# Cross attention in rounds of two query tiles on unnormalised queries, the forget chain inside a branch projection, the output turned chunk by chunk, and six fewer filler products in a climb

## The chip, the cores and the metric

The kernel runs on one core of a Trainium2 chip. Five engines work side by side, each through its own instruction list, and hold each other back with semaphores only: TensorE (PE, matrix products and transposes into the PSUM banks; its weight loads are PEld), VectorE (DVE), ScalarE (ACT), GpSimd (POOL) and SyncE (SP, which issues the loads). The metric is the device time of one execution in microseconds (us), as the median of several runs; lower is better.

## The reference

A two-layer decoder trunk over 512 tokens of width 1024, in float32. A layer adds three things to x: the gated sum of four token mixers, a cross attention into 256 memory rows, and a SwiGLU feed-forward part. Each is RMS-normalised before and after. What the change touches is this:

```python
def rmsnorm(x, g):
    xf = x.astype(jnp.float32)
    y = xf * lax.rsqrt(jnp.mean(xf * xf, axis=-1, keepdims=True) + NORM_EPS)
    return (y * g.astype(jnp.float32)).astype(x.dtype)

def fox_mixer(q, k, v, f_logit, f_bias):      # one of the four mixers
    log_f = jax.nn.log_sigmoid(f_logit.astype(jnp.float32) + f_bias.astype(jnp.float32))
    cum = jnp.cumsum(log_f, axis=1)
    return causal_block_attention(q, k, v, HEAD_DIM ** -0.5, cum)   # scores + cum[t] - cum[s]

def memory_cross_attention(h, mem_n, w_q, w_kv, w_o):
    B, S, _ = h.shape
    M = mem_n.shape[1]
    q = (h @ w_q).reshape(B, S, XA_HEADS, HEAD_DIM)                 # 4 heads of 64
    kv = (mem_n @ w_kv).reshape(B, M, 2, XA_HEADS, HEAD_DIM)
    s = jnp.einsum('bshd,bmhd->bhsm', q, kv[:, :, 0]).astype(jnp.float32) * HEAD_DIM ** -0.5
    p = jax.nn.softmax(s, axis=-1)
    o = jnp.einsum('bhsm,bmhd->bshd', p.astype(kv.dtype), kv[:, :, 1])
    return o.reshape(B, S, XA_HEADS * HEAD_DIM) @ w_o

for l in range(DEPTH):
    h = rmsnorm(x, mix_norm_pre[l])
    ...   # four mixers, fox_mixer the last of them
    merged = sum(jax.nn.sigmoid(h @ w_gate[l, i]) * (y @ w_branch[l, i]) for i, y in enumerate(branches))
    x = x + rmsnorm(merged @ w_out[l], mix_norm_post[l])
    hx = rmsnorm(x, xa_norm_pre[l])
    y = memory_cross_attention(hx, rmsnorm(mem, xa_mem_norm[l]), xa_w_q[l], xa_w_kv[l], xa_w_o[l])
    x = x + rmsnorm(y, xa_norm_post[l])
    ...   # SwiGLU part, its norms and residual
return x
```

## The kernel before

**Data.** The residual stream lies in `trunk` with features on partitions: eight chunks of 128 features by 512 tokens. Every float32 product is made of three products of rounded parts (high by high, low by high, high by low; `product`), so whatever enters a product is first split: ACT writes the rounded high part (`w_hi`, `h_hi`, `q_tile`, `p_hi`, `y_hi`), DVE then the difference (`w_lo`, `h_lo`, `p_lo`, `y_lo`).

**Weights.** All projections are cut into units of 128 by 1024 weights. SP loads a unit into one of two slots of `w_f32`; `next_unit(name, k)` on ACT and on DVE splits the unit that follows unit k of that name (the lists of all units are one sequence). A slot is split again only once PE has used the unit two before. PE accumulates in two banks `acc`, in turn, and a bank has to be read before it is written again. The order of PE, of ACT and of DVE is written out by hand, engine by engine; each runs strictly in that order.

**Climb.** `climb` is the stretch in which a residual is being added chunk by chunk (DVE: scale, add, then the low part; ACT: the high part and the square) while PE already projects the chunks that are ready: first unit of chunk kt, second unit of chunk kt-2, and the sums of squares (`chunk_sums`, products with one column). `keep_busy(n)` puts n products of 128x512 with no use between them. There are six climbs; the one of layer 0's first norm goes by another path (`paired_sums`).

**Cross attention.** It is the pass `XA` of `attend`: 16 steps, a head by a tile of 128 queries each. A step is: scores (PE, 3 products of 256 columns), bias and row minimum in one DVE operation, exp with row sum (ACT), reciprocal and division (DVE), two transposes (PE), high part (ACT), low part (DVE), application to the values (PE, 6 products of 128 columns). Ahead of it the norm's factor is spread over 128 rows (`spread_rows`), copied (`copy_rows`), multiplied into the projected queries (`by_rows`, into `proj_x`), and those are split (`stage`). The queries are negated, so a row's minimum takes the place of its maximum.

**Forget chain.** After the projection `fox` and ahead of its attention, DVE and ACT make the running sums of log sigmoid: eight DVE operations and, on ACT, an exp and a log, on 8 rows of 512. ACT then splits a weight unit and the first head.

**Branch.** `branch(b)` multiplies a mixer's output by w_branch in four units of two chunks; DVE, per unit, makes the next unit's `w_lo`, and twice takes a bank times the gate (bank free from here) and adds it to `trunk`.

**Output.** At the end `trunk` is turned to token order in eight half tiles (a tile of tokens needs all eight chunks), ACT copies each, SP writes out a tile of tokens (512 KB, rows of 4 KB) at a time.

## Time and profile before

| | |
|---|---|
| time, median of 3 runs | 2554.49 us (2554.11 to 2559.22) |
| the profiled execution's own time | 2556.63 us |
| its span, first to last instruction | 2554.9 us |
| PE busy | 2436.2 us, 95% of the span |
| DVE busy | 1507.8 us, 59% |
| ACT busy | 1138.6 us, 45% |
| POOL busy | 113.7 us, 4% |
| mean granted TensorE clock | 0.983 of full speed |

The span is taken from one profiled execution; its own time is 1.7 us above the span. PE is busy nearly all the time, so the stretches in which it isn't, or works without use, are what other orders can win or lose.

### The profile page before, as it was taken

To read this page: it belongs to the slowest core of one execution; us is meant where nothing else is said; L and a number is where in the kernel's file an instruction comes from. 1 tells how busy PE (TensorE), PEld (TensorE's weight loads), DVE (VectorE), ACT (ScalarE), POOL (GpSimd) and SP (SyncE) were. 2 spreads that over 40 slices of the span, in tenths; PEclk is the share of its full clock that TensorE was granted. 3 is DMA by queue.
4 is the path that set the end of the run, shared out by engine and by line. 5 is a ranking of instruction groups with operands and counts; after the bars stand their busy time and mean duration, and the time that the engine had idled before them with its cause. 6 is when DMAs were issued, how large, how long until landed. Compare 5 with 4: busy or idle time off the path is not lost.

```text
span 2554.9 us, 37831 instructions
## 1 busy us (share of the span) xinstructions
PE 2436.2 (95%) x13433; PEld 2015.8 (79%) x13433; DVE 1507.8 (59%) x3235; ACT 1138.6 (45%) x2267; POOL 113.7 (4%) x179
## 2 busy tenths in 40 slices
PE   6998999999999899999999999999999998999998
PEld 4887787888878688888878877878878787888886
DVE  5668776772775555552275786768447556555422
ACT  4456564643545532222243565646346445222322
POOL 3000000000001100000010000000000101000000
PEclk8999999999999999999999999999999999999999
DMA  5321122123124023333332212221321320333332
GB/s 120 91 91 34 50 67 67 59 62 95 42 81 134 28 64 92 97 98 91 89 83 71 79 34 58 67 67 50 83 74 50 124 74 26 91 99 98 95 91 70
DMA packets 343961, 193.99 MB, mean 76 GB/s; under 512 B 29825, under 2 KB 339206, under 8 KB 343174
## 3 DMA queue, kind: packets, MB, share of 16 engines
q1 hardware_dynamic: 340512, 178.02, 24.4%
q0 software_dynamic: 2224, 13.67, 1.5%
q8 instruction: 90, 1.47, 0.2%
q10 hardware_dynamic: 1078, 0.36, 0.1%
q14 instruction: 57, 0.47, 0.1%
HBM read 184.69 MB, written 7.34 MB: 75 GB/s over the span
## 4 chain that ended last, share of the span: by engine, by line
PE 82%; DVE 8%; ACT 4%; issue 4%; POOL 1%; DMA 0%; DVEq 0%; POOLq 0%; ACTq 0%
PE acc L1272 62%; PE o_acc L1272 5%; PE turn L1482 3%; PE scores L1272 3%; PE turn L1272 2%; ACT w_hi L800 2%; PE scores L1332 1%; DVE ring L2091 1%; DVE w_lo L1809 1%; PE o_acc L1382 1%; PE scores L1467 1%; DVE p_lo L1932 1%; PE scores L1468 1%; PE scores L1527 1%; PE scores L1472 1%
## 5 line engine op out<-in xcount | busy, mean ns | idle before, releaser
L1809 DVE TENSOR_TENSOR w_lo<-w_f,w_hi 128x1024 fp32r<-128x1024 f32 x336 | 411.6, 1225 | 552.1 <-ACT w_hi L800 551.6
L1272 PE MATMUL acc<-h_hi,w_hi 128*128 128x512 f32 x1680 | 666.3, 397 | 8.4 <-DVE h_lo L1853 4.8
L1272 PE MATMUL acc<-h_hi,w_lo 128*128 128x512 f32 x1680 | 660.2, 393 | 0.0
L1272 PE MATMUL acc<-h_lo,w_hi 128*128 128x512 f32 x1680 | 660.1, 393 | 0.0
L800 ACT ACTIVATE w_hi<-w_f 128x1024 fp32r<-128x1024 f32 x336 | 354.2, 1054 | 285.3 <-PE acc L1272 258.2
L1272 PEld LDWEIGHTS acc<-h_hi,w_hi 128*128 128x128 f32 x1680 | 318.3, 189 | 70.7 <-issue 10.5
L1272 PEld LDWEIGHTS acc<-h_hi,w_lo 128*128 128x128 f32 x1680 | 317.8, 189 | 66.2
L1272 PEld LDWEIGHTS acc<-h_lo,w_hi 128*128 128x128 f32 x1680 | 318.4, 190 | 58.3
L856 ACT ACTIVATE p_hi<-turn 128x128 fp32r<-128x128 f32 (+3 forms) x356 | 149.9, 421 | 271.4 <-PE turn L1482 269.3
L1932 DVE TENSOR_TENSOR p_lo<-turn,p_hi 128x128 fp32r<-128x128 f32 (+3 forms) x356 | 166.0, 466 | 73.8 <-ACT p_hi L856 72.6
L944 ACT ACTIVATE ring<-ring,neg_max 128x128 f32<-128x128 f32 (+2 forms) x352 | 189.6, 539 | 38.5 <-DVE neg_max L2091 37.7
L1272 PE MATMUL o_acc<-p_hi,v_hi 128*64 128x128 f32 x816 | 189.5, 256 | 7.8 <-DVE p_lo L1932 7.6
L1482 PE MATMUL turn<-ident,ring 128*128 128x128 f32 x816 | 150.9, 278 | 30.4 <-DVE ring L2110 17.4
L1482 PEld LDWEIGHTS turn<-ident,ring 128*128 128x128 f32 x816 | 102.8, 141 | 83.3 <-issue 55.3
L1272 PE MATMUL o_acc<-p_lo,v_hi 128*64 128x128 f32 x816 | 164.1, 225 | 0.0
L1272 PE MATMUL o_acc<-p_hi,v_lo 128*64 128x128 f32 x816 | 163.6, 224 | 0.0
L1272 PE MATMUL acc<-y_hi,w_hi 128*128 128x512 f32 x360 | 146.3, 406 | 3.6 <-ACT wide L1078 1.4
L1272 PE MATMUL acc<-y_lo,w_hi 128*128 128x512 f32 x360 | 144.4, 401 | 0.0
L1272 PE MATMUL acc<-a_hi,w_lo 128*128 128x512 f32 x352 | 138.7, 394 | 0.0
L1272 PE MATMUL acc<-a_hi,w_hi 128*128 128x512 f32 x352 | 138.7, 394 | 0.0
L1272 PE MATMUL acc<-a_lo,w_hi 128*128 128x512 f32 x352 | 138.7, 394 | 0.0
L1272 PEld LDWEIGHTS o_acc<-p_hi,v_hi 128*64 128x64 f32 x816 | 111.6, 137 | 21.4 <-DVE p_lo L1932 12.6
(351 smaller groups left out, 3846.3 us busy)
## 6 DMA issues: line engine op xcount, KB each, us to landing
w_f<-in_ffn_w_in_dram SPq DMA_DIRECT2D x88, 512.0 KB, 3.8
w_f<-in_w_gate_dram SPq DMA_DIRECT2D x64, 512.0 KB, 4.0
w_f<-in_w_in_dram SPq DMA_DIRECT2D x62, 512.0 KB, 3.8
w_f<-in_w_branch_dram SPq DMA_DIRECT2D x32, 512.0 KB, 3.5
w_f<-in_ffn_w_out_dram SPq DMA_DIRECT2D x32, 512.0 KB, 4.0
w_f<-in_w_out_dram SPq DMA_DIRECT2D x16, 512.0 KB, 4.1
w_f<-in_ffn_w_out_dram SPq DMA_DIRECT2D x16, 384.0 KB, 3.4
x_spill<-trunk POOLq DMA_DIRECT2D x2, 2048.0 KB, 6.8
```

What stands on the lines that cost most here:

```text
L800: nc.scalar.activation(w_hi[:, u % 2, :], w_f32[:, u % 2, :], ACT.Copy).then_inc(w_high, 1)
L856: nc.scalar.activation(dst, src, ACT.Copy).then_inc(turn_high, 1)
L944: nc.scalar.activation(ring[:, s % RING, 0:w], ring[:, s % RING, 0:w], ACT.Exp, bias=neg_max[:, s % 4:s % 4 + 1], scale=-1.0, accum_out=ro ...
L1272: ins = nc.tensor.matmul(dst, a, b, start=(n == 0 and not added), stop=(n == count - 1))
L1332: ins = nc.tensor.matmul(SUMS[:, i:i + 1], squares[:, c % 2, i * P:(i + 1) * P], ones[:, 0:1], start=(c == 0 and i == 0), stop=(c == n - 1 ...
L1382: nc.tensor.matmul(o_acc[0][:, :].rearrange("p (t f) -> p t f", t=NT), ident_r[:, :], ident_r[:, :].unsqueeze(1).to_broadcast([P, NT, P]), ...
L1467: nc.tensor.matmul(bank, halves, k[0], start=True, stop=False)
L1468: nc.tensor.matmul(bank, halves, k[1], start=False, stop=True).then_inc(scored, 1)
L1472: nc.tensor.matmul(bank, pick[:, h:h + 1].to_broadcast([P, P]), cum_rows[:, k0:k0 + w], start=True, stop=False)
L1482: ins = nc.tensor.transpose(bank[0:w, t * P:(t + 1) * P], ring[:, s % RING, t * w:(t + 1) * w], ident[:, :])
L1809: nc.vector.tensor_tensor(w_lo[:, u % 2, :], w_f32[:, u % 2, :], w_hi[:, u % 2, :].bitcast(F32), ALU.subtract).then_inc(w_ready, 1)
L1932: nc.vector.tensor_tensor(dst, bank, high.bitcast(F32), ALU.subtract).then_inc(turn_ready, 1)
```

## The change

Four parts.

1. **Cross attention** gets functions of its own, `cross_attend`. The queries are split straight from the projection's bank, without the norm's factor; that factor enters as the scale of the exp, per row, and in its bias (`x_neg` = minus the factor, `x_bias` = the row's minimum times the factor). `spread_rows`, `copy_rows` and `by_rows` fall away there. A round takes two tiles of queries: 8 rounds in place of 16 steps; the (zero) bias is no longer added, the minimum is a plain reduction, and one broadcast multiplication divides both tiles.
2. **Forget chain**: the exp and the log stand in ACT's list behind the first unit split of branch 2, DVE's eight operations stand in three pieces between the four bodies of branch 2. The loops of that branch on ACT and DVE are written out.
3. **Output**: turned chunk by chunk (four tiles of a chunk), each when its chunk is ready, into `proj`; SP writes chunks 0 to 3, then 4 and 5, then 6, then 7 (row pieces of 2 KB, 1 KB, 512 B, 512 B).
4. **Filler products**: in a climb (but layer 0's first) 7 in place of 13: 4 and 3 behind the sums of chunks 0 and 1, none behind the others.

```diff
@@ climb (PE) @@
-                    keep_busy(1)
-                    if not paired_sums:
+                    if paired_sums:
+                        keep_busy(1)
+                    else:
                         chunk_sums(l, name, kt)
                         if kt < lag:
-                            keep_busy(3 - kt)
+                            keep_busy(4 - kt)
                 for kt in range(KT - lag, KT):
                     terms(second, kt)
                 if name == "xa_pre":
-                    spread_rows(l, name)
+                    pe.sem_inc(rbc_ready, 1)
@@ cross_attend (PE) @@
+                def score(u):
+                    h, j = divmod(u, 2)
+                    if j == 0:
+                        pe.wait_ge(qk_ready, l * NIT + (IB["xa"] + h + 1))
+                    if u >= 2:
+                        pe.wait_ge(x_exped, st + (u - 1))
+                    ...   # 2 tiles x 3 products of 256 columns
+                def turn_pair(u):
+                    bank = turn_bank(l, "xa", 0, u)
+                    pe.wait_ge(x_divided, st + (u + 1))
+                    ...   # 4 transposes
+                def apply(u):
+                    ...   # waits head_done, turn_ready; 6 products of 256 columns
+                values(0, 2)
+                pe.wait_ge(ms_ready, l * NNORM + NB_OF["xa_pre"] + 1)
+                score(0)
+                for u in range(XSTEPS + 2):
+                    if u + 1 < XSTEPS:
+                        score(u + 1)
+                    if 1 <= u <= XSTEPS:
+                        turn_pair(u - 1)
+                    if u >= 2:
+                        apply(u - 2)
@@ cross_attend (ACT) @@
+                def exps(u):
+                    ...
+                        ins = nc.scalar.activation(ring[:, u % RING, cols], scores[u % 2][:, cols], ACT.Exp,
+                                                   bias=x_bias[:, c:c + 1], scale=x_neg[:, t:t + 1],
+                                                   accum_out=row_sum[:, c:c + 1])
+                stage(0)
+                stage(1)
+                next_unit(l, "xq", 1, 0)
+                value_turns(l, "v_xa", 2, P, MT)
+                for u in range(XSTEPS + 3):
+                    if u in (2, 4):
+                        stage(u // 2 + 1)
+                    if u < XSTEPS:
+                        exps(u)
+                    if 1 <= u <= XSTEPS:
+                        high(u - 1)
+                    if u >= 4 and u % 2 == 0:
+                        out_high_part(u // 2 - 2)
@@ cross_attend (DVE) @@
+                for u in range(XSTEPS + 4):
+                    if u < XSTEPS:
+                        least(u)
+                        shift(u)
+                    if u == 0:
+                        next_unit(l, "xq", 1, 0)
+                    if 1 <= u <= XSTEPS:
+                        divide(u - 1)
+                    if 2 <= u <= XSTEPS + 1:
+                        turn_rest(l, "xa", 0, u - 2, p_lo[:, u % 2, :], turn[(TB["xa"] + u) % 2][:, :], p_hi[:, u % 2, :])
+                    if u in (2, 4):
+                        stage(u // 2 + 1)
+                    if u >= 5 and u % 2 == 1:
+                        out((u - 5) // 2)
@@ branch 2 (ACT) @@
+                elif b == 2:
+                    for k in range(4):
+                        next_unit(l, "br2", k, 0)
+                        if k == 0:
+                            act.wait_ge(forget, l * 8 + 2)
+                            nc.scalar.activation(exp_neg, logit, ACT.Exp, scale=-1.0).then_inc(forget_act, 1)
+                            act.wait_ge(forget_act, l * 2 + 1)
+                            nc.scalar.activation(softplus, exp_neg, ACT.Ln, bias=1.0).then_inc(forget_act, 1)
@@ branch 2 (DVE) @@
+                elif b == 2:
+                    body(0, 0)
+                    forget_logits(l)
+                    body(1, 0)
+                    forget_sums(l)
+                    body(2, 0)
+                    forget_halves(l)
+                    body(3, 0)
@@ output (SP, PE) @@
+            for c0, c1 in ((0, 4), (4, 6), (6, 7), (7, 8)):
+                cols = slice(c0 * P, c1 * P)
+                sp.wait_ge(s_act, KT + c1)
+                sp.dma_start(out[0].rearrange("(t p) d -> p t d", p=P)[:, :, cols], out_tok[:, :, cols]).then_inc(s_out, 16)
...
-            pe.wait_ge(trunk_new, L * NRS + KT)
+            for c in range(KT):
+                pe.wait_ge(trunk_new, trunk_at(L - 1, "ffn_post", c))
```

How this moves instructions is read from the order of each engine's list. First, ACT's list of the kernel before around the start of the fox attention: the exp and the log (`proj<-proj 8x512`) stand behind the fox projection (`proj<-acc,evac_scale`) and ahead of the weight split and of the first head's high parts.

```order
L811 ACTIVATE proj<-acc,evac_scale 128x512
L549 REGISTER_ALU
L549 COMPARE_AND_BRANCH
L1189 ACTIVATE proj<-proj 8x512
L1191 ACT_TABLE_LOAD
L1191 ACTIVATE proj<-proj 8x512
L800 ACTIVATE w_hi<-w_f 128x1024
L933 ACTIVATE k_hi<-proj 128x512
L935 ACTIVATE q_tile<-proj 64x512
```

ACT's list of the changed kernel around the start of branch 2: the last head's high part of the MLA attention, the split of branch unit 1, then the chain, then the splits of units 2, 3 and of fox's first.

```order
L980 ACTIVATE y_hi<-o_acc 64x512
L816 ACTIVATE w_hi<-w_f 128x1024
L1146 ACTIVATE proj<-proj 8x512
L1148 ACT_TABLE_LOAD
L1148 ACTIVATE proj<-proj 8x512
L816 ACTIVATE w_hi<-w_f 128x1024 x3
```

So the chain now stands ahead of the split of branch unit 2. On DVE, in the changed kernel, the body of branch unit 0, `forget_logits` and the body of unit 1 follow each other:

```order
L1933 TENSOR_TENSOR w_lo<-w_f,w_hi 128x1024
L2414 SCALAR_TENSOR_TENSOR ring<-wide,acc 128x512
L2419 TENSOR_TENSOR trunk<-trunk,ring 128x512
L2414 SCALAR_TENSOR_TENSOR ring<-wide,acc 128x512
L2419 TENSOR_TENSOR trunk<-trunk,ring 128x512
L2375 TENSOR_SCALAR proj<-narrow,f_bias 8x512
L2378 SCALAR_TENSOR_TENSOR proj<-proj 8x512
L2380 TENSOR_SCALAR proj<-proj 8x512
L2381 MEMSET cum_rows 128x512
L1933 TENSOR_TENSOR w_lo<-w_f,w_hi 128x1024
L2414 SCALAR_TENSOR_TENSOR ring<-wide,acc 128x512
```

The low part of branch unit 2 (the second `w_lo`) and the reading of unit 1's first bank (the last row) now stand behind four chain operations. In the cross attention, DVE's list before, for two steps:

```order
L2091 ISA ring,neg_max<-scores,mask 128x256
L2091 ISA neg_max 128x1
L2106 RECIPROCAL over_sum<-row_sum 128x1
L2110 TENSOR_SCALAR ring<-ring,over_sum 128x256
L1932 TENSOR_TENSOR p_lo<-turn,p_hi 128x256
L2091 ISA ring,neg_max<-scores,mask 128x256
L2091 ISA neg_max 128x1
L2106 RECIPROCAL over_sum<-row_sum 128x1
L2110 TENSOR_SCALAR ring<-ring,over_sum 128x256
L1932 TENSOR_TENSOR p_lo<-turn,p_hi 128x256
```

and in the changed kernel, for one round, which is the same two tiles:

```order
L2332 TENSOR_REDUCE neg_max<-scores 128x2
L2325 SCALAR_TENSOR_TENSOR x_bias<-neg_max,x_neg 128x2
L2339 RECIPROCAL over_sum<-row_sum 128x2
L2342 TENSOR_TENSOR ring<-ring,over_sum 128x512
L2056 TENSOR_TENSOR p_lo<-turn,p_hi 128x512
```

Ten operations of one tile became five of two tiles.

## Rows read from the trace of the kernel before

**Rows 1.** The page's head and its PE line: busy time, share, instructions.

```profile
span 2554.9 us, 37831 instructions
PE 2436.2 (95%) x13433; PEld 2015.8 (79%) x13433; DVE 1507.8 (59%) x3235; ACT 1138.6 (45%) x2267; POOL 113.7 (4%) x179
```

**Rows 2.** Stretches: busy PE, PEld, DVE, ACT, POOL; granted clock (1.00 full), DMA, GB/s.

```profile
643.70:647.20 3.50, 3.50 (x16) 3.04 (x14) 2.35 (x6) 2.63 (x4) 0.00 (x0) 0.51 0.01 2
818.30:841.60 23.30, 22.92 (x135) 19.48 (x133) 14.96 (x24) 9.93 (x16) 1.01 (x1) 1.00 0.16 51
841.70:845.10 3.40, 0.66 (x4) 0.42 (x4) 2.75 (x4) 2.88 (x6) 0.00 (x0) 1.00 0.00 0
845.10:855.40 10.30, 8.81 (x45) 7.88 (x46) 7.64 (x31) 5.04 (x17) 0.00 (x0) 0.50 0.19 54
```

**Rows 3.** Timeline, layer 0's climb into cross attention, chunks 6 and 7 (start, duration, engine).

```profile
832.56 0.39 PE L1382 MATMUL o_acc<-ident_r 128*128 128x512 f32 x1
833.82 0.75 DVE L1889 SCALAR_TENSOR_TENSOR h_lo<-trunk,gains,h_hi 128x512 fp32r<-128x512 f32 x1 [0.79 <-ACT h_hi L843]
835.08 0.40 PE L1382 MATMUL o_acc<-ident_r 128*128 128x512 f32 x1
835.32 0.95 PE L1332 MATMUL scores<-ones,ring 128*128 128x1 f32 x8
```

**Rows 4.** Timeline, layer 0's cross attention, from the climb's last product to the output projection.

```profile
839.88 0.40 PE L1272 MATMUL acc<-h_hi,w_lo 128*128 128x512 f32 x1
...
845.84 0.58 PE L1272 MATMUL scores<-k_hi,q_tile 128*128 128x256 f32 x1 [1.49 <-DVE q_tile L2080]
...
847.46 0.51 ACT L944 ACTIVATE ring<-ring,neg_max 128x256 f32<-128x256 f32 x1 [1.61 <-DVE neg_max L2091]
...
877.77 0.39 PE L1272 MATMUL acc<-y_hi,w_hi 128*128 128x512 f32 x1
```

**Rows 5.** DVE groups by shape: count, busy us, mean ns, idle before.

```profile
L2106 DVE RECIPROCAL over_sum<-row_sum 128x1 f32<-128x1 f32 x288 | 45.5, 158 | 17.8 <-ACT ring L944 17.3
L2110 DVE TENSOR_SCALAR ring<-ring,over_sum 128x256 f32<-128x256 f32 x112 | 39.6, 354 | 3.9
...
L1998 DVE TENSOR_TENSOR ring<-ring,cmp_over 128x512 f32<-128x512 f32 x4 | 2.8, 691 | 0.1
...
L1979 DVE TENSOR_REDUCE cmp_least<-ring 128x16 f32<-128x512 f32 x4 | 2.7, 686 | 0.1
```

**Rows 6.** Timeline, layer 0's branch 2: its third unit's split, a body's end, that unit's start.

```profile
552.32 1.06 ACT L800 ACTIVATE w_hi<-w_f 128x1024 fp32r<-128x1024 f32 x1 [1.87 <-PE acc L1272]
...
553.96 0.69 DVE L2182 TENSOR_TENSOR trunk<-trunk,ring 128x512 f32 x1
...
558.24 0.39 PE L1272 MATMUL acc<-y_hi,w_hi 128*128 128x512 f32 x1
```

**Rows 7.** Timeline, layer 0's forget chain and the start of the fox attention.

```profile
632.45 0.47 DVE L2396 TENSOR_SCALAR proj<-narrow,f_bias 8x512 f32<-8x512 f32 x1
...
635.72 0.61 ACT L1189 ACTIVATE proj<-proj 8x512 f32<-8x512 f32 x1
...
638.18 1.04 ACT L800 ACTIVATE w_hi<-w_f 128x1024 fp32r<-128x1024 f32 x1
...
642.77 0.33 PE L1472 MATMUL scores<-cum_rows,pick 128*128 128x128 f32 x1 [3.05 <-DVE q_tile L2080]
```

**Rows 8.** Timeline, the output: last chunk added, first copy, last write issued.

```profile
2543.99 0.69 DVE L1902 TENSOR_TENSOR trunk<-trunk,ring 128x512 f32<-128x512 f32 x1
...
2545.89 0.60 ACT L1256 ACTIVATE wide<-turn 128x512 f32<-128x512 f32 x1 [16.28 <-PE turn L1790]
...
2551.86 0.33 SPq L666 DMA_DIRECT2D out_dram<-wide  x1
```

**Rows 9.** DMA issues: KB each, median us from issue to landing.

```profile
w_f<-in_w_in_dram SPq DMA_DIRECT2D x62, 512.0 KB, 3.8
...
w_f<-in_mla_w_kv_up_dram SPq DMA_DIRECT2D x4, 256.0 KB, 2.7
```

More of the change, by code:

```diff
@@ L383, in build @@
         divided = sem("divided")
+        x_scored = sem("x_scored")
+        x_least = sem("x_least")
+        x_rstd = sem("x_rstd")
+        x_shift = sem("x_shift")
+        x_exped = sem("x_exped")
+        x_over = sem("x_over")
+        x_divided = sem("x_divided")
+        x_applied = sem("x_applied")
         out_high = sem("out_high")
@@ L2162, in attend, with cross_attend, stage, mean @@
                         nsa_rest((s - 13) // 8)
+            def cross_attend(l):
+                st = l * XSTEPS
+                def stage(n):
+                    dve.wait_ge(q_high, l * NIT + (IB["xa"] + n + 1))
+                    if n % 2 == 0:
+                        wait_chunk(dve, l, "xq", n // 2, 0, 0)
+                    own, at = XA.half(n), 2 * (n % 2)
+                    if n % 2 == 0:
+                        k = n // 2 % 2
+                        nc.vector.tensor_tensor(k_lo[:, k, 0:M], proj_x[:, PJ_K["xa"] + n // 2, 0:M],
+                                                k_hi[:, k, 0:M].bitcast(F32), ALU.subtract)
+                    nc.vector.scalar_tensor_tensor(q_tile[own, at + 1, :], acc[(CB["xq"] + n // 2) % 2][own, :],
+                                                   -(HD ** -0.5), q_tile[own, at, :].bitcast(F32), ALU.mult,
+                                                   ALU.subtract).then_inc(qk_ready, 1)
+                def mean():
+                    dve.wait_ge(token_sums, l * NNORM + NB_OF["xa_pre"] + 1)
+                    nc.vector.tensor_scalar(mean_sq[:, 0:NT], SUMS[:, 0:NT], 1.0 / D, EPS, ALU.mult,
+                                            ALU.add).then_inc(ms_ready, 1)
+                    dve.sem_inc(summed, 1)
+                def root():
+                    dve.wait_ge(rstd_ready, l * NNORM + NB_OF["xa_pre"] + 1)
+                    nc.vector.tensor_scalar(x_neg[:, :], rstd[:, 0:NT], -1.0, None, ALU.mult).then_inc(x_rstd, 1)
+                    dve.sem_inc(rstd_high, 1)
+                    dve.sem_inc(rstd_split, 1)
+                def shift(u):
+                    c, t = slice(u % 2 * 2, u % 2 * 2 + 2), u % 2 * 2
+                    dve.wait_ge(x_rstd, l + 1)
+                    dve.wait_ge(x_least, st + (u + 1))
+                    nc.vector.scalar_tensor_tensor(x_bias[:, c], neg_max[:, c], -1.0, x_neg[:, t:t + 2], ALU.mult,
+                                                   ALU.mult).then_inc(x_shift, 1)
+                def least(u):
+                    c = u % 2 * 2
+                    dve.wait_ge(x_scored, st + (u + 1))
+                    nc.vector.tensor_reduce(neg_max[:, c:c + 2], pair_columns(scores[u % 2][:, :]), mybir.AxisListType.X,
+                                            ALU.min).then_inc(x_least, 1)
+                def divide(u):
+                    c = slice(u % 2 * 2, u % 2 * 2 + 2)
+                    dve.wait_ge(x_exped, st + (u + 1))
+                    nc.vector.reciprocal(over_sum[:, c], row_sum[:, c]).then_inc(x_over, 1)
+                    dve.wait_ge(x_over, st + (u + 1))
+                    p = pair_columns(ring[:, u % RING, :])
+                    nc.vector.tensor_tensor(p, p, over_sum[:, c].unsqueeze(2).to_broadcast([P, 2, M]),
+                                            ALU.mult).then_inc(x_divided, 1)
+                def out(h):
+                    dve.wait_ge(out_high, l * NOUT + (OB["xa"] + h + 1))
+                    rows = XA.half(h)
+                    nc.vector.tensor_tensor(y_lo[rows, h // 2, :], o_acc[h % 2][0:HD, :], y_hi[rows, h // 2, :].bitcast(F32),
+                                            ALU.subtract).then_inc(head_done, 1)
+                stage(0)
+                mean()
+                stage(1)
+                value_turns(l, "v_xa", 2, P, MT)
+                root()
+                for u in range(XSTEPS + 4):
[12 more added lines that the diff above has]
+                        out((u - 5) // 2)
```

159 lines of the change are left out of this document (101 added, 58 removed).

## The prediction

> **What bounds the kernel now.** I began with the page's head: PE is busy for 95% of the span [rows 1], so time can only come from stretches where PE stands still, multiplies without use, or runs slow. I looked for these in three views. The list of waits names, for PE, the starts of both attentions and the output. The busy time by stretch gives the granted clock: full in the climb, but 0.50 for 10.3 us in the cross attention and 0.51 for 3.5 us at the start of the fox attention, each time after a stretch in which PE did little (0.66 us of 3.40 before the cross attention's) [rows 2]. These are the two levels, 2.4 and 1.2 GHz. Last, the timeline around each edit. Both layers show the same pattern within 0.1 us, so I work out layer 0 and double it.
>
> **Filler products.** In the climb a chunk costs PE 2.52 us (832.56 to 835.08) [rows 3]. The difference of two starts, not the 0.39 us shown, is what a product costs in a stream: 0.23 us. Each climb loses six, 1.4 us. Does PE then run into DVE? DVE ends the low part of the last chunk at 834.57; PE takes it up some 0.8 us after 835.32, at 836.1 [rows 3]. Five fillers less bring that to 834.95, still behind DVE. So all of it counts: 5 climbs x 1.4 = **7.0 us**. If PE met DVE early it would be 4; if the clock fell, see the rivals.
>
> **Cross attention, the entry.** Before, the last climb product starts at 839.88, the first score at 845.84, the first exp at 847.46 [rows 4]: 7.6 us of spreading, copying, scaling and splitting. After, the first queries' bank is full before the second's, and ACT and DVE split it while PE still climbs. Behind the climb's end (838.7, with the 1.4 us) stand only two groups of value transposes (0.45), six score products (0.69), a pipeline lag of 0.3, a reduction over 512 (0.69) and two small operations (0.2 each; the reciprocal's 0.158 is the nearest [rows 5]). The factor itself, which POOL makes, lies beside these. First exp: about 841.4. That is 6.1 us earlier, 1.4 of them counted already.
>
> **Cross attention, the rounds.** From the first exp to the output projection's second part it is 30.3 us now (847.46 to 877.77) [rows 4]. After, DVE has per round a reduction 0.69, a broadcast division 0.69, a low part 0.69 [rows 5] and two small operations of 0.2: 2.45 us, times 8 = 19.6. Add the splits of heads 2 and 3 (1.65), three heads' output splits (2.0) and a weight split (1.2): 24.4 us from 840.4, hence the last `p_lo` at 864.8. Then the last application (0.7, and lags), six useful products and six fillers (2.8), under which the last head's split lies: 868.5. ACT needs some 1.9 us per round for two exps and a high part, PE 1.8 us at full clock, so DVE is the bound, as long as the clock is full. At 1.2 GHz PE would need 3.6. PE idles for 3.5 us before the first transposes, so I expect a low stretch again, and since rows 2 show the present one lasting 10.3 us, I add 0.6. In all 877.8 - 869.1 = 8.7 us, 7.3 without the fillers' part: 2 x 7.3 = **14.6 us**. Bounds: the entry alone (4.7 a layer, 9.4) and no low clock with overlaps at their best (8.5 a layer, 17).
>
> A rule weighed here. The division of one tile takes 0.354 us as a TENSOR_SCALAR of 256, the broadcast TENSOR_TENSOR of 512 takes 0.691 [rows 5], so two tiles cost 0.71 before and 0.69 after. The Trainium skill (VectorE: DVE Perf Modes, The perf-mode tier table) says that in fp32 a tensor_scalar runs at twice the rate of a tensor_tensor, and that a tensor_reduce has only the single rate. By that rule alone the division would double, from 8 x 0.71 to 11 us a layer, and the whole edit would be worth some 5 us less a layer; by the rows fixed cost makes up for the rate at this width, and I go by the rows.
>
> **Forget chain, what it frees.** Before, ACT starts the exp at 635.72 and comes to the weight split at 638.18, 2.5 us later; the first fox score starts at 642.77 after PE waited 3.05 us [rows 7]. Without the chain ACT and DVE split the first head at once, and the score is ready when PE has done its ahead products, near 639.6. The low clock of 643.7 to 647.2 [rows 2] should go with the hole; it costs up to 1.7 us. Partly the value splits come late then, so I take **3.9 us** a layer, between 3.0 and 4.9.
>
> **Forget chain, what it costs.** Its new place is not free. ACT's exp needs the second of DVE's chain operations, and DVE starts them after the body of unit 0, which ends at 554.65 [rows 6]; at 0.47 for the first [rows 7] and about 0.69 for the second, ACT begins at 555.8 and reaches the next weight split 2.5 us later, at 558.3. That is the split of unit 2, which ACT now does at 552.32 and PE needs at 558.24 [rows 6]. ACT ends it at 559.35, DVE its low part at 560.6, and behind that in DVE's list stands the reading of unit 1's first bank (0.7), without which PE may not begin unit 2: 561.35. **PE waits 3.1 us** where it waits nothing now. What is queued behind it, unit 3, waits no more: DVE's next pieces (1.9 and 1.1 us) lie under PE's 5.6 us per unit. This hole is as long as the one at the fox attention, so I expect a low clock behind it too, in a stretch that PE alone bounds: 1.7 us. In all 4.9 us lost, 3.9 won: 2 x 1.0 = **2.0 us slower**. Bounds: both layers 7.8 faster (all hidden) to 3.8 slower.
>
> **Output.** The last chunk is added at 2544.68; the first copy to follow starts at 2545.89, since the transposes take 1.2 us, and takes 0.60. Seven more half tiles pass before the last write is issued at 2551.86; the span ends at 2554.9, 3.0 later [rows 8], [rows 1]. After, only the last chunk's transposes and copy follow, so that its write goes out at 2546.5. The chunks before come every 1.4 us and fit beneath. The last write is 256 KB in pieces of 512 B: a load of 256 KB took 2.7 us, one of 512 KB in such pieces 3.8 [rows 9], the last write of before 3.0. I take 2.9: end at 2549.4, **5.4 us** saved (4.5 to 5.6).
>
> **Sum.** 7.0 + 14.6 + 5.4 - 2.0 = 25.0 us. The profiled span of 2554.9 becomes 2529.9, its own time of 2556.6 becomes 2531.6; that execution is 2.1 above the median of 2554.49, so the forecast for the median is **2529.5**. The many low-clock stretches shift against the work when everything ahead moves; a few may come or go at 1.7 us each, so +-3.
>
> **Rivals.** *The branch hides the chain.* If DVE or ACT have more slack there than I read, only the gain stays: 7.8 faster in place of 2.0 slower, 2519.7. For it speaks that DVE is idle for over a microsecond per unit there; against it that ACT's split of unit 2 is tied to the log. 12%.
>
> *The rounds gain nothing.* Half as many rounds make each round's chain longer, with fewer rounds in flight. If the rounds stay at 30 us, only the entry remains: 2534.7. For it: DVE's time per pair of tiles hardly falls, the wins are overlaps and the low clock. 18%.
>
> *The clock falls in the climbs.* The fillers may be what holds the clock at 1.00 there [rows 2]. A climb has 48 products of 512 columns, 11.2 us at full clock; at 1.2 GHz through the whole climb that adds 11 us each, 56 in five, against 25.0 won: 2585.5, slower. It decides from about two fifths of the climbs' time (25 of 56). For it: the clock did fall after stretches with little work. Against it: there PE stood still, while here it never does, and per chunk 1.4 us of dense products stay beside 0.8 us of one-column ones (before 1.63 beside 0.8). 3%.
>
> *The rounds don't do what they say.* The exps straight from the PSUM bank hold it longer and scores wait for them, so that nothing is gained in the cross attention, entry included: 2544.1. 3%.
>
> **How the numbers follow.** My forecast has 64%, its own range 2524 to 2535. Leaving 2 in 10 out, and with the bounds of the chain, of the rounds and of the clock, 2519 to 2539. A measurement of this kernel can tell about 0.2%, 5.1 us, from no change. Faster by more than that: all cases but the clock's and half of what I have not thought of: 94%; within: 3%; slower: 3%.
>
> **What would show it.** PE's waits between the climb and the cross attention gone, the 3.05 us before the fox score gone, and in their place one of about 3 us in branch 2, at the first product of its third unit, released by DVE. Cross attention from the climb's end to the output projection near 30 us against 37.7. Rounds at 2.4 to 3.1 us with DVE busy over 85%. The clock 1.00 in all climbs. The last write issued 1.9 us after the last chunk is added. Wrong would be the forecast if the wait in branch 2 isn't there, if DVE waits inside the rounds, or if the clock falls in a climb.

## The result, and the profile after

The changed kernel takes 2515.93 us (median of 4, 2515.32 to 2516.88) against 2554.3 (2553.88 to 2559.22): a ratio of 0.9843 with a 95% interval of 0.9832 to 0.9855, 38 us less. Forecast were 2529.5 and a range down to 2519.0. The direction was right, the size was not: 13.6 us more were won than the sum said, outside the range. The profiled spans tell the same (2554.9 to 2513.6, 41.3 us less, where the sum had 25.0).

The page's head of the changed kernel, beside [rows 1]:

```profile
span 2513.6 us, 37293 instructions
PE 2401.8 (96%) x13291; PEld 1999.9 (80%) x13291; DVE 1499.2 (60%) x3149; ACT 1133.2 (45%) x2249; POOL 113.9 (5%) x179
```

PE does 142 products fewer, of which 30 are fillers of 512 columns and the rest lies in the cross attention, and is busy 34.4 us less: 0.24 us for each, more than even a filler's 0.23. That is a first sign of something that the sum had missed, though what PE spends at the low clock is in this number too.

**Cross attention.** Timeline of the changed kernel, from the climb's last product to the output projection's second part (compare [rows 4]):

```profile
834.27 0.40 PE L1343 MATMUL acc<-h_hi,w_lo 128*128 128x512 f32 x1
...
837.07 0.56 ACT L1032 ACTIVATE ring<-scores,x_bias,x_neg 128x256 f32<-128x256 f32 x1 [1.49 <-DVE x_bias L2325]
...
838.42 0.36 PE L1343 MATMUL scores<-k_hi,q_tile 128*128 128x256 f32 x1 [1.89 <-ACT ring L1032]
...
864.08 0.39 PE L1343 MATMUL acc<-y_hi,w_hi 128*128 128x512 f32 x1
```

From the climb to the first exp it is 2.80 us where it was 7.58, from there to the output projection's second part 27.01 where it was 30.31. One round of it on DVE:

```profile
851.25 0.67 DVE L2332 TENSOR_REDUCE neg_max<-scores 128x2 f32<-128x512 f32 x1
852.02 0.16 DVE L2325 SCALAR_TENSOR_TENSOR x_bias<-neg_max,x_neg 128x2 f32<-128x2 f32 x1
852.10 0.16 DVE L2339 RECIPROCAL over_sum<-row_sum 128x2 f32<-128x2 f32 x1
852.29 0.69 DVE L2342 TENSOR_TENSOR ring<-ring,over_sum 128x512 f32<-128x512 f32 x1
852.90 0.68 DVE L2056 TENSOR_TENSOR p_lo<-turn,p_hi 128x512 fp32r<-128x512 f32 x1
```

The next reduction starts at 853.51, 2.26 us after this one; the forecast had 2.45 for a round's operations. Of the signs that the prediction named, one of the wrong ones did appear once: DVE waits 1.18 us inside the rounds, for `p_hi`, in the stretch at low clock shown below.

**Forget chain.** DVE's pieces, ACT's chain and PE's wait in branch 2 of the changed kernel (compare [rows 6, 7]), and PE at the start of the fox attention:

```profile
551.82 0.47 DVE L2375 TENSOR_SCALAR proj<-narrow,f_bias 8x512 f32<-8x512 f32 x1
...
553.03 0.63 ACT L1146 ACTIVATE proj<-proj 8x512 f32<-8x512 f32 x1 [5.04 <-DVE proj L2378]
...
555.51 1.99 ACT L816 ACTIVATE w_hi<-w_f 128x1024 fp32r<-128x1024 f32 x2
...
557.73 0.68 DVE L2414 SCALAR_TENSOR_TENSOR ring<-wide,acc 128x512 f32<-128x512 f32 x1
...
558.55 0.47 PE L1343 MATMUL acc<-y_hi,w_hi 128*128 128x512 f32 x1 [2.84 <-DVE ring L2414]
...
639.80 0.22 PE L1544 MATMUL scores<-cum_rows,pick 128*128 128x128 f32 x1
```

The wait is where it was forecast, at the branch's third unit, released by DVE's reading of the bank, 2.84 us long (3.1 forecast). The first fox score starts at 639.80 with no wait before it. But behind the branch's wait the clock did not fall, in either layer of this kernel. Busy time by stretch, changed kernel (columns as in [rows 2]); the first row is the branch's third unit, the second the rounds of the cross attention, the third the one low stretch inside them:

```profile
558.50:564.10 5.60, 5.55 (x24) 4.43 (x24) 5.50 (x8) 0.00 (x0) 0.00 (x0) 1.00 0.36 94
838.40:862.70 24.30, 18.98 (x122) 15.64 (x123) 20.39 (x45) 16.82 (x44) 0.00 (x0) 0.93 0.08 23
857.70:861.30 3.60, 3.41 (x16) 2.95 (x17) 1.67 (x3) 1.07 (x2) 0.00 (x0) 0.53 0.00 0
```

**Output.** The last chunk's add, transposes and copy, and the writes:

```profile
2507.85 0.69 DVE L2026 TENSOR_TENSOR trunk<-trunk,ring 128x512 f32<-128x512 f32 x1
...
2508.60 0.66 PE L1914 MATMUL turn<-ident,trunk 128*128 128x128 f32 x4 [0.73 <-DVE trunk L2026]
...
2509.29 0.60 ACT L1327 ACTIVATE proj<-turn 128x512 f32<-128x512 f32 x1 [0.79 <-PE turn L1914]
...
2504.38 5.98 SPq L682 DMA_DIRECT2D out_dram<-proj  x4
```

From the end of that add to the end of the span it is 5.06 us, where it was 10.22 [rows 1, 8]. The last write is issued at 2509.92, 1.4 us after the add (1.9 forecast), and the span ends 3.7 us later (2.9 forecast).

**Where nothing was changed.** The FFN's output projection is untouched by the diff. A chunk of it is 66 products of 512 columns, and ACT squares each chunk as it is done. Two of these operations in a row, first of the kernel before, then of the changed one:

```profile
1167.99 0.60 ACT L834 ACTIVATE ring<-acc 128x512 f32<-128x512 f32 x1 [3.08 <-PE acc L1272]
1183.39 0.60 ACT L834 ACTIVATE ring<-acc 128x512 f32<-128x512 f32 x1 [3.08 <-PE acc L1272]
```

```profile
1153.60 0.60 ACT L850 ACTIVATE ring<-acc 128x512 f32<-128x512 f32 x1 [2.96 <-PE acc L1343]
1168.56 0.60 ACT L850 ACTIVATE ring<-acc 128x512 f32<-128x512 f32 x1 [2.96 <-PE acc L1343]
```

15.40 us before, 14.96 now, with the clock at 1.00 in both: 0.2333 us a product against 0.2267. This is 3.5 us a layer where the sum had nothing. Looking back, the trace of before shows both rates side by side: products that move `h_hi` and `h_lo` start 0.2267 us apart, those that move the `v`, `y` and `a` tiles 0.2333. After, all start 0.2267 apart.

### The profile page after: what moved, and what is told of

Read it like the earlier page. It is cut to its first block, busy times and chain, and to the rows that moved or that the text cites. A ratio compares the mean times of both kernels' runs of the same rounds, so it can differ in the third digit from the quotient of the medians.

```text
span 2513.6 us, 37293 instructions
## 1 busy us (share of the span) xinstructions
PE 2401.8 (96%) x13291; PEld 1999.9 (80%) x13291; DVE 1499.2 (60%) x3149; ACT 1133.2 (45%) x2249; POOL 113.9 (5%) x179
## 4 chain that ended last, share of the span: by engine, by line
PE 82%; DVE 9%; ACT 4%; issue 4%; POOL 1%; DVEq 0%; POOLq 0%; ACTq 0%
PE acc L1343 63%; PE o_acc L1343 5%; PE turn L1554 3%; PE scores L1343 2%; PE turn L1343 2%; ACT w_hi L816 2%; DVE w_lo L1933 1%; PE scores L1403 1%; DVE p_lo L2056 1%; DVE ring L2215 1%; PE scores L1539 1%; PE o_acc L1453 1%; PE scores L1540 1%; PE scores L1653 1%; PE scores L1544 0%
## 5 line engine op out<-in xcount | busy, mean ns | idle before, releaser
L1343 PE MATMUL o_acc<-p_hi,v_hi 128*64 128x128 f32 (+1 forms) x784 | 183.5, 257 | 7.3 <-DVE p_lo L2056 7.3
L960 ACT ACTIVATE ring<-ring,neg_max 128x128 f32<-128x128 f32 (+2 forms) x320 | 172.7, 540 | 32.1 <-DVE neg_max L2215 31.6
L1343 PE MATMUL o_acc<-p_lo,v_hi 128*64 128x128 f32 (+1 forms) x784 | 159.0, 226 | 0.0
L1343 PE MATMUL o_acc<-p_hi,v_lo 128*64 128x128 f32 (+1 forms) x784 | 158.3, 225 | 0.0
L1554 PE MATMUL turn<-ident,ring 128*128 128x128 f32 x752 | 136.1, 275 | 22.8 <-DVE ring L2236 12.6
L1554 PEld LDWEIGHTS turn<-ident,ring 128*128 128x128 f32 x752 | 94.9, 140 | 72.5 <-issue 45.5
L1343 PEld LDWEIGHTS o_acc<-p_hi,v_hi 128*64 128x64 f32 x784 | 106.4, 136 | 20.4 <-DVE p_lo L2056 12.6
```

The lines of the kernel that those rows point to most:

```text
L960: nc.scalar.activation(ring[:, s % RING, 0:w], ring[:, s % RING, 0:w], ACT.Exp, bias=neg_max[:, s % 4:s % 4 + 1], scale=-1.0, accum_out=ro ...
L1343: ins = nc.tensor.matmul(dst, a, b, start=(n == 0 and not added), stop=(n == count - 1))
L1554: ins = nc.tensor.transpose(bank[0:w, t * P:(t + 1) * P], ring[:, s % RING, t * w:(t + 1) * w], ident[:, :])
```

## The experiments

The diff has one edit that no step of the prediction spoke of: `x_neg` and `x_bias`, two tiles of 32 bytes per partition as laid out, are declared among the small tiles. Everything declared behind them lies 64 bytes further: `p_hi`, `v_hi`, `y_hi`, `a_hi` and what follows. The weight tiles and `h_hi`, `h_lo` are declared ahead and stay. The first theory (A) was that a moving operand is read faster from a better place of its own; its rival (B) that order or neighbours made the difference.

### Where the tiles lie

**before_64**, the kernel before with the shift alone:

```diff
         neg_max = sb("neg_max", [P, 4])
+        sb("gap", [P, 16])
```

> The kernel before with one unused tile of 64 bytes per partition behind neg_max, where the changed kernel has its two new small tiles; nothing else differs. Theory A (place in memory): a product of 512 columns whose moving operand (y_hi, y_lo, a_hi, a_lo, the v and y tiles that hold the first norm's result) begins 64 bytes off a multiple of 128 takes 0.2333 us in a stream, one that begins on it 0.2267; the shift puts all of them on it. 8 FFN output chunks a layer at 0.44 us less each (3.5 a layer), four branches at 0.49 (2.0 a layer) and about 1 a layer at the first norm: 12 to 14 us less, 2541 us, and the spacing in the FFN output becomes 0.2267. Theory B (the order, or what runs beside them, made these products faster): 2554, spacing 0.2333 as before.

2546.79 us, ratio 0.9956 (0.9943 to 0.9969) to the kernel before, whose median beside it was 2557.19: 10.4 us less, and 8 to 15 by the interval. The span is 2543.0, 11.9 less than the profiled span of before; that compares two single executions. The FFN's chunks, in the same view:

```profile
1163.76 0.60 ACT L835 ACTIVATE ring<-acc 128x512 f32<-128x512 f32 x1 [2.96 <-PE acc L1273]
1178.72 0.60 ACT L835 ACTIVATE ring<-acc 128x512 f32<-128x512 f32 x1 [2.96 <-PE acc L1273]
```

14.96 us, from an unused tile. B is out: the place makes the difference.

**after_64**, the changed kernel shifted by 64 bytes more (the same line behind `x_bias`):

> The changed kernel with one unused tile of 64 bytes per partition behind its two new tiles, which takes every tile behind them back to 64 bytes off a multiple of 128. Theory A: 12 to 14 us slower than the changed kernel, 2529 us, spacing 0.2333 in the FFN output. Theory B: 2516, spacing 0.2267.

2520.37 us, ratio 0.9853 (0.984 to 0.9866); span 2519.0. Slower, but by 4 to 5 us and not by 12 to 14, and the spacing is a third one, 15.11 / 66 = 0.2289:

```profile
1154.41 0.60 ACT L851 ACTIVATE ring<-acc 128x512 f32<-128x512 f32 x1 [3.00 <-PE acc L1344]
1169.52 0.60 ACT L851 ACTIVATE ring<-acc 128x512 f32<-128x512 f32 x1 [3.00 <-PE acc L1344]
```

**before_32** (`[P, 8]` in place of `[P, 16]`):

> The kernel before with an unused tile of 32 bytes per partition at the same place: the tiles behind it begin 96 bytes past a multiple of 128, 32 past one of 64. If only a start on a multiple of 128 is fast: spacing 0.2333 or more, 2554 or more. If the crossing of a boundary is what costs, by how far the start is off: between. Theory B: 2554 with the spacing as before.

2558.91 us, ratio 1.0002 (0.9993 to 1.0011). The spacing stays at 0.2333, the time with it.

**w_64**, the weights alone:

```diff
         w_f32 = sb("w_f32", [P, 2, 1024])
+        sb("gap_a", [P, 16])
         w_hi = sb("w_hi", [P, 2, 1024], F32R)
         w_lo = sb("w_lo", [P, 2, 1024], F32R)
+        sb("gap_b", [P, 16])
```

> The kernel before with 64 unused bytes ahead of w_hi and w_lo and 64 behind them: only these two, the operands that TensorE loads as weights, now begin 64 bytes off a multiple of 128 (all else keeps its remainder). If the start counts for the moving operand alone: 2554 and spacings as before. If it counts for loaded weights too: some 7200 products with weights from them by up to 0.007 us, up to 48 us slower, and a longer weight load than 0.189 us.

2550.39 us, ratio 0.9974 (0.9962 to 0.9987), span 2545.8. None of the listed outcomes. The products of `h` went from 0.2267 to 0.229, and those of `a`, `v`, `y` from 0.2333 to 0.2267, though only the weights had changed their place against 128. Theory A falls: `a_hi` was slow at one remainder in before and fast at the same remainder here. What fits all four is the distance from the weight tile to the moving tile (theory C).

**all_64**, everything from the weights on further by 64, all distances kept (only the first of the two lines above):

> The kernel before with 64 unused bytes ahead of w_hi, w_lo, h and all that follows: every tile named so far is 64 bytes further, and the distance between the weights and the moving operands is what it was in the kernel before. Theory A as first stated (the moving operand's own place): a, v, y products at 0.2267, h products slower than 0.2267. Theory C, made after w_64 (the distance from the weight tile to the moving tile decides, by its remainder to 256: 0 gives 0.2267, 64 gives 0.229, 192 and 224 give 0.2333): h at 0.2267, a, v, y at 0.2333, time as before.

2556.2 us, ratio 0.9996 (0.9986 to 1.0005); spacings 0.2267 for `h` and 0.2333 for the rest. C said this, A the opposite. This is the cleanest pair against A: the `a`, `v` and `y` tiles lie at the same place here as in before_64, yet are slow here and fast there; only the weights lie elsewhere.

**order_128**, the two small tiles `neg_max` and `row_sum` declared ahead of `w_hi`:

> The kernel before with two of its small tiles (neg_max and row_sum, 32 bytes each as laid out) declared ahead of w_hi: weights and h 64 bytes further, all tiles behind the small ones where they were. The distance from the weights to a, v and y is then 128 by its remainder to 256, to h 0 as before. Theory C with the remainder to 128 deciding between good and bad: a, v, y at 0.2267, some 12 us less than before. Theory C with the remainder to 256 deciding: between 0.229 and 0.2333, 0 to 8 us less. Theory A (the moving operand's own place): 0.2333 as before and h above 0.2267.

2558.11 us, ratio 1.0006 (0.9996 to 1.0015); 0.2333 for `a`, 0.2325 for `v` and `y`, 0.2267 for `h`. A distance of 128 is no better than 192. All distances seen, as remainders to 256, with the median spacing of products of 512 columns in dense streams at a clock of 1.00:

| distance, weight tile to moving tile | spacing, us | seen in |
|---|---|---|
| 0 | 0.2267 | `h` in all but w_64; `a`, `v`, `y` in before_64, w_64, the changed kernel |
| 64 | 0.229 | `a`, `v`, `y` in after_64; `h` in w_64 |
| 128 | 0.2325 to 0.2333 | order_128 |
| 192 | 0.2333 | before, all_64 |
| 224 | 0.2333 | before_32 |

The Trainium skill (TensorE: Matmul & The Clock Gate, Back-to-back issue gap) gives 512/2.4 + 2.5, that is 216 ns, for the isolated gap at this width, and about 131 ns for a sustained stream of weight loads and products. The best spacing here is 226.7 ns, so the measurement decides.

### The four parts

**rounds_only**: the changed kernel with 13 fillers, the chain behind the fox projection and the old output, so that the cross attention and the shift remain.

```diff
-            for c0, c1 in ((0, 4), (4, 6), (6, 7), (7, 8)):
+            for t in range(NT):
...
-                            keep_busy(4 - kt)
+                            keep_busy(3 - kt)
...
                 project(l, "fox")
+                forget_logits(l)
+                forget_sums(l)
+                forget_halves(l)
```

> The changed kernel with the old output, 13 fillers and the old chain: what is left of the change is the cross attention in rounds, with its two new small tiles, which shift the tiles behind them by 64 bytes. By the prediction's term 14.6 us faster than before (2540). By the theory of the place in memory the shift adds 12 to 14: 2526 to 2528. Measured against before_64, which has the shift alone, the rounds by themselves should give 14 to 17.

2526.19 us, ratio 0.9879 (0.9854 to 0.9903), span 2527.1: 15.9 under before_64's span. By these two executions that is the worth of the rounds over the whole run; forecast were 14.6. It is not a sharp number: by the ratios, 0.9956 and 0.9879, it would be 19.7, give or take 7, since the profiled execution of rounds_only was the slowest of its four. The timeline is sharper. In layer 0 the climb's last product starts at 837.62, the first exp at 840.41, the projection's second part at 867.20: 2.8 and 26.8 us, against 7.58 and 30.31 in the kernel before, so 8.3 us less in this layer.

**fill13**: the first of the undone parts alone (13 fillers).

> The changed kernel with the 13 filler products per climb again (five climbs). By the prediction's sum 7.0 us slower than the changed kernel (2523), with the climb into cross attention at 2.52 us per chunk; by the profile after, where the climbs came out 1.2 us shorter each, 6.0. Rival: the fillers hid behind DVE in some climbs, 4 us.

2519.54 us, ratio 0.9862 (0.9839 to 0.9884), span 2517.1. Against the changed kernel's span 3.5 slower. From the sums of chunk 0 to those of chunk 7 the five climbs take 18.50, 18.05, 18.04, 18.49 and 18.04 us, against 17.56, 16.88, 16.86, 17.56 and 16.87 in the changed kernel: together 5.4 slower. In the rest of the run this execution had about 3 us less at the low clock. Here is how the climb looks in the changed kernel (sums of chunks 1, 2, 3 and 7):

```profile
817.16 0.95 PE L1403 MATMUL scores<-ones,ring 128*128 128x1 f32 x8
820.28 0.95 PE L1403 MATMUL scores<-ones,ring 128*128 128x1 f32 x8
823.12 0.95 PE L1403 MATMUL scores<-ones,ring 128*128 128x1 f32 x8
...
832.21 0.94 PE L1403 MATMUL scores<-ones,ring 128*128 128x1 f32 x8
```

Chunks 4 to 7 take 2.27 us each ((832.21 - 823.12) / 4), 0.25 less than in [rows 3]. Chunk 2 takes 3.12 and chunk 3 2.84, as in the kernel before: there PE waits for DVE, which makes a weight's low part at 818.19, and a filler less is not felt. So four of six count in the two climbs into the cross attention; in the three others only chunk 2 is as slow as it was, and five count: 2 x 0.92 + 3 x 1.15 = 5.3 us, which is what the climbs show.

**old_output**: the second alone.

> The changed kernel with the old output (turned by tiles of tokens behind the last chunk). By the prediction 5.4 us slower than the changed kernel, by its profile (5.1 us from the last added chunk to the end, against 10.2) 5.1: 2521. Rival: other things at the end, nothing.

2520.38 us, ratio 0.9867 (0.9843 to 0.9891). The last stretch of the run, from a wait of PE early in layer 1's FFN to the end, is 6.2 us longer than in the changed kernel (365.02 against 358.82), with more of it at the low clock; the 10.22 - 5.06 = 5.16 us of the profiles are the output's own.

**old_chain**: the third alone.

> The changed kernel with the forget chain back behind the fox projection. By the prediction 2.0 us faster than the changed kernel (2514): the wait of 3 us and a low clock in branch 2 go, the wait at the fox start comes back. By the profile after, in which no low clock follows the wait of 2.84 us in branch 2: 1.3 us a layer slower, 2518.5.

2517.66 us, ratio 0.9852 (0.9829 to 0.9875), span 2517.3. The sum had it faster than the changed kernel; it is not. I compare the stretch that holds branch 2, the fox projection and the fox attention, from PE's wait for `ring` near the end of the MLA attention (543.88 in before) to the same wait in the fox attention (731.05):

| kernel | layer 0 | at low clock | layer 1 | at low clock |
|---|---|---|---|---|
| before_64 (old chain) | 186.50 | 3.4 | 187.61 | 6.8 |
| rounds_only (old chain) | 187.56 | 6.8 | 187.70 | 6.8 |
| old_chain | 187.61 | 6.8 | 187.79 | 6.8 |
| changed kernel | 185.36 | 0 | 185.36 | 0 |
| fill13 | 185.35 | 0 | 186.80 | 3.4 |
| early | 184.54 | 0 | 184.53 | 0 |
| late | 182.59 | 0 | 182.61 | 0 |

Against old_chain the changed kernel wins 2.25 and 2.43 us, 4.7 in all, where the prediction had the new place lose 2.0. But this is won in granted clock. The wait itself only moved, from 3.05 to 2.84 us, and in old_chain 6.8 us at low clock go with it. The rows of fill13, whose chain stands in the new place, show that the new wait can be followed by a low stretch as well (PE at the branch's third unit in layer 1, and the stretch behind it with its granted clock, 0.50):

```profile
1792.26 0.47 PE L1343 MATMUL acc<-y_hi,w_hi 128*128 128x512 f32 x1 [2.87 <-DVE ring L2413]
```

```profile
1792.70:1796.10 3.40, 3.40 (x10) 2.65 (x9) 3.33 (x6) 0.00 (x0) 0.00 (x0) 0.50 0.61 154
```

With 3.4 us at low clock on both sides the old place takes 186.50 (before_64, layer 0) and the new one 186.80 (fill13, layer 1): no gain. Over the eight kernels with the old chain the wait of 3.05 us had a low stretch with it in 14 of 16 cases (eight of 3.4 us, six of 6.8); over the changed kernel, after_again, after_64, fill13 and old_output the wait of 2.8 us had one in 2 of 10. So the new place does better by how often the clock falls, and the 4.7 us are not a fixed price. The ratios (0.9852 and 0.9843, with intervals that overlap) do not tell the two apart.

### A better place for the chain

**after_again**, the changed kernel once more, for comparison with the next ones:

> The changed kernel, unaltered, beside the next ones on one chip, as what they are compared with. 2516, 1.5 to 1.6% under the kernel before.

2515.71 us, ratio 0.9832 (0.9819 to 0.9845).

**early**:

```diff
-                    body(0, 0)
                     forget_logits(l)
+                    body(0, 0)
```

> The changed kernel with the first four DVE operations of the forget chain one place earlier, ahead of the body of branch 2's unit 0, so that ACT's exp and log run at 549 to 551.5 and not at 553 to 555.5, before PE frees the weight slot at 552.3. Theory: PE's wait of 2.84 us at the branch's third unit goes and no other comes, 5.7 us less than the changed kernel (2510). Rival: the body of unit 0 is then 2 us late and PE waits for its bank at unit 1 instead, or the low part of unit 1 comes late; no gain or part of it.

2513.87 us, ratio 0.9823 (0.9807 to 0.984): not told apart from the changed kernel by its time. The table has 0.8 us a layer. The rival had it: PE now waits one unit earlier, for a body that the chain made late.

```profile
554.40 0.47 PE L1343 MATMUL acc<-y_hi,w_hi 128*128 128x512 f32 x1 [2.67 <-DVE ring L2414]
```

**late**:

```diff
                         next_unit(l, "br2", k, 0)
-                        if k == 0:
+                        if k == 1:
                             act.wait_ge(forget, l * 8 + 2)
```

> The changed kernel with ACT's exp and log one weight split later in branch 2, behind the split of its third unit; DVE's pieces stay. Theory: the chain cost the changed kernel only because the split of the third unit was queued behind the log; now that split runs when PE frees its slot (near 552.5), the exp and log lie between it and the fourth, and PE's wait of 2.84 us at the branch's third unit shrinks to 0.3 us or less (DVE's four operations, 2.0 us, remain ahead of the low part). 5 us less than the changed kernel (2511). Rival: DVE's operations alone keep most of the wait (1.5 us or more), 2513.

2508.45 us, ratio 0.9803 (0.9789 to 0.9817), the fastest version of all. ACT, from the split of the third unit to that of the fourth, and PE at the first product of the third unit:

```profile
550.73 1.06 ACT L816 ACTIVATE w_hi<-w_f 128x1024 fp32r<-128x1024 f32 x1 [1.87 <-PE acc L1343]
553.90 0.63 ACT L1146 ACTIVATE proj<-proj 8x512 f32<-8x512 f32 x1 [2.11 <-DVE proj L2378]
...
556.67 1.06 ACT L816 ACTIVATE w_hi<-w_f 128x1024 fp32r<-128x1024 f32 x1 [0.19 <-PE acc L1343]
...
556.67 0.47 PE L1343 MATMUL acc<-y_hi,w_hi 128*128 128x512 f32 x1
```

The wait of 2.84 us is gone: the product before this one starts at 556.18, so that 0.49 us lie between the two, 0.23 of which is the spacing in a stream. The stretch is 2.77 us shorter in layer 0 and 2.75 in layer 1, with no low clock on either side. So the wait came from ACT's order alone: the split was queued behind the log. DVE's four operations, 2.0 us ahead of the same low part, cost next to nothing.

### Fewer fillers still

**fill0** (on early) and **late_fill0** (on late):

```diff
                         if kt < lag:
-                            keep_busy(4 - kt)
+                            keep_busy(0)
```

> As early, and no filler products at all in the five climbs. Theory of the prediction (what PE leaves out counts until it meets DVE, and DVE needs some 2.2 us per chunk of a climb): chunks 0 and 1 then wait for DVE, so at most 1 us less a climb, 0 to 5 us less than early. Rival of the prediction (the fillers hold the clock): low clock in each climb, 1.7 us for each stretch in which it falls, 8 us more or worse.

2510.86 us, ratio 0.9812 (0.9799 to 0.9825), against early's 0.9823.

> As late, without filler products in the five climbs. In fill0 the clock fell in both climbs into cross attention, where chunks 0 and 1 without fillers leave PE waiting for DVE, and in none of the other three. Theory: the same again here; the three other climbs win 0.3 to 0.5 us each, those two lose 2: within 3 us of late. Rival: fewer fillers help everywhere, 4 us less than late.

2510.08 us, ratio 0.9812 (0.9799 to 0.9826), against late's 0.9803. The times do not tell the pairs apart, and they differ in sign. What happens is seen in the climb into the cross attention of layer 0 in fill0, the sums of chunks 1 to 3, and a stretch of it with its granted clock:

```profile
816.91 0.95 PE L1403 MATMUL scores<-ones,ring 128*128 128x1 f32 x8
821.06 1.70 PE L1403 MATMUL scores<-ones,ring 128*128 128x1 f32 x8
825.32 1.11 PE L1403 MATMUL scores<-ones,ring 128*128 128x1 f32 x8
```

```profile
818.00:826.00 8.00, 7.55 (x26) 6.10 (x26) 7.61 (x12) 3.34 (x6) 0.00 (x0) 0.57 0.21 68
```

Chunk 1 takes 2.13 us of which PE's work is 1.5, so PE waits for DVE there as well, and in this climb the clock fell in all four cases (both layers of fill0 and of late_fill0); chunks take 4.2 us in place of 3.12 and 2.84. The mildest is layer 1 of late_fill0:

```profile
2049.10:2052.50 3.40, 3.17 (x9) 2.56 (x10) 3.27 (x6) 1.24 (x2) 0.00 (x0) 0.50 0.24 43
```

From the sums of chunk 0 to those of chunk 7 these four climbs take 19.8, 20.0, 21.8 and 18.0 us, against 17.5 to 17.6 with seven fillers. In the three other climbs the clock did not fall in any of six cases, and they win 0.5 us each. So the seven fillers left earn their place in the climbs into the cross attention, as far as four cases show it, and not in the others.

## Why the prediction was off, step by step

The spans, kernel by kernel: before 2554.9; with the shift 2543.0 (11.9); with the rounds 2527.1 (15.9); with fillers, chain and output 2513.6 (13.5). Each is one execution, and the runs of the kernel before beside before_64 alone lie between 2549.75 and 2563.39, so these steps are good to a few us. The last three terms by themselves add up to 15.3. By term:

| term | forecast | measured |
|---|---|---|
| tiles shifted by 64 bytes | not in the sum | 11.9 in the spans, 10.4 in the medians |
| cross attention | 14.6 | 15.9 in the spans, 8.3 a layer in layer 0's timeline |
| fillers | 7.0 | 5.4 in the climbs, 3.5 in the spans |
| forget chain | -2.0 | 4.7, of it granted clock nearly all |
| output | 5.4 | 5.2 |

**The step that failed** is the sum itself, "7.0 + 14.6 + 5.4 - 2.0 = 25.0 us": it costs what the four parts do and takes for granted that what isn't edited runs as before. The two new tiles change the distance between the weights and the moving operands, and some 2,100 products of 512 columns in the FFN's output projection and the branches, besides those of the first norm and some projections, each got up to 0.0067 us faster, 14 us if all of it reached the end. This is shown: a kernel with the shift alone wins it, one with the shift and 64 bytes more loses part of it, and one with all distances kept changes nothing. The trace of before held the two rates, and I read over them by taking 0.23 for both.

**The second is the chain's low clock.** "PE waits 3.1 us" was right (2.84 at that place). "I expect a low clock behind it too" was wrong for the changed kernel, where the clock stayed at 1.00, and came true in 2 of the 10 cases of that wait; the stretch is then 1.45 us longer (186.80 against 185.35 in fill13). "I take 3.9 us a layer" for what it frees fits the low stretch of 3.4 us in [rows 2]: from before_64's layer 0 to late it is 186.50 - 182.59 = 3.9. Where the low stretch is 6.8 us long, from old_chain to late, it is 5.0 and 5.2, above the upper bound of 4.9. So 5.0 to 5.2 won and 2.8 lost are the 2.3 of the table, and the step that failed was to charge the clock as a fixed 1.7 us behind either hole. Why a hole of 3.05 us at the fox start nearly always had a low stretch with it and one of 2.84 in the branch seldom, no run here settles. The fox start has a second wait of 0.97 us ahead of its own, which the branch has not; that this is the reason is only argued.

**Cross attention.** The entry was right (4.8 us against 4.7), the rounds a bit better than forecast (3.3 to 3.5 against 2.6). DVE is busy 84% of the rounds (20.39 of 24.30 us, "over 85%" was the forecast), PE 78% and ACT 69%, which fits DVE as their bound; no run tests it. The broadcast division took 0.69 us, as the rows said. The doubling that the prediction drew from the Trainium skill (VectorE: DVE Perf Modes, The perf-mode tier table) did not come: 8 x 0.69 = 5.5 us a layer, where 16 single divisions took 5.7. The low stretch of 10.3 us in [rows 2] shrank to one of about 3.4.

**Fillers.** The estimate of DVE was right at the last chunk, but I looked only there. At chunk 2, and before the cross attention at chunk 3, PE waits for DVE in both kernels, so that four or five fillers of six count: 5.4 us where the sum had 7.0.

**Output.** Right within 0.3 us, with some luck: the last write was issued 0.5 us sooner after the add than forecast and took 0.8 us longer to end.

**The rivals.** That the clock falls in the climbs did not come true with seven fillers, yet it did with none, in the climbs into the cross attention: the mechanism is there, and the change stopped short of it. That the branch hides the chain became true in late only. The chances given to the forecast and the four rivals add up to 100%, which left nothing for a cause outside the five, and the largest error came from there.

## What to carry to other kernels

- Before summing what a diff does, ask what it moves in memory. A new small tile among the first ones shifts all behind it, and here that was worth as much as any edit but one. Where a product's spacing differs between operands at the same width and clock, try a gap of 32 to 224 bytes: it costs one line.
- A step moved into another engine's shadow is queued behind what its engine has to do next: put it behind the split or load that others wait for, never ahead. One line's place was worth 2.8 us a layer.
- Undo parts one by one and compare stretches between two fixed waits, not only whole times: 0.8 and 2.8 us a layer repeated there within 0.1 us, while the medians left them open. Read the granted clock of both stretches with it: the chain's 2.3 us repeated in both layers too, and was nearly all clock.

## What the hardware showed unexpectedly

TensorE's rate in a dense stream of weight load and product (128 x 128 by 512 columns, float32 of rounded parts, clock 1.00) depended on the distance in bytes between the weights' tile and the moving tile: 0.2267 us at a remainder of 0 to 256, 0.229 at 64, 0.2325 to 0.2333 at 128, 192 and 224. Neither tile's own place mattered in the places tried. What in the chip collides is not shown. A remainder of 32, 96 or 160 wasn't tried.

Whether the clock falls with a wait of PE was not fixed by the wait's length here. The same wait of 3.05 us had no low stretch with it in 2 cases, one of 3.4 us in 8 and one of 6.8 us in 6; a wait of 2.8 us had one of 3.4 us in 2 of 10.
